# Two-layer hybrid encoder step on one core: the norms' sums taken by token, root and inverse on 128x5, the factors spread by the identity

## The chip, the core and the metric

The kernel runs on one core of a Trainium2 chip. The core's engines run their own instruction streams and meet at semaphores: TensorE (PE, with its weight loads shown apart as PEld), VectorE (DVE), ScalarE (ACT), GpSimd (POOL), and SyncE (SP), which issues the weight transfers. The metric is the device time of one launch in microseconds; before the change the median of three runs is 3305.26 us (3304.61 to 3308.02).

## The reference, cut to what matters

One inference step of a two-layer encoder over 512 prompt tokens and 64 sample tokens, 576 in all, with 1024 features. All in float32.

```
def rmsnorm(x, g):
    y = x * lax.rsqrt(jnp.mean(x * x, axis=-1, keepdims=True) + EPS)
    return y * g
# each of 2 layers:
h = x + 0.5 * rmsnorm(swiglu_1(rmsnorm(x)))           # FFN 1, inner width 2816
u = rmsnorm(h);  branch inputs, gate logits = u @ w_in
#   A  GLU -> causal depthwise conv (31) -> LayerNorm -> swish
#   B  HGRN2 gated linear recurrence; rmsnorm over each head's 64 features, * silu(g)
#   C  sliding-window attention      D  stick-breaking attention
y_n = o_n @ w_branch[n];  mix = (sum_n sigmoid(gate_n) * y_n) @ w_out
h = h + rmsnorm(mix)
h = h + 0.5 * rmsnorm(swiglu_2(rmsnorm(h)))           # FFN 2
h = h + rmsnorm((p @ ple_w) * sigmoid(rmsnorm(h) @ ple_gate_w))   # PLE
```

## The kernel before, in words

**Tiling.** Features lie on the partitions and tokens on the free axis: an activation is eight tiles of 128x576 (`KD = 8`, `T = 576`), and a pair of PSUM banks holds one tile as two halves of 288 (`pair(p)`), or as 512 + 64 (`flat(p)`). Every weight is streamed in units of 128x1024: SP brings `wraw`, ACT rounds it to `whi` (L551), POOL subtracts for the rest `wlo` (L1936), and PE makes three products of each 128x128 block with each half of a tile, high by high, high by low and low by high (`products`, L589).

**Norms.** Each layer has eight RMS norms over the 1024 features. The even ones (`norm_h`: F1PRE, MPRE, F2PRE, PPRE) take the residual `h`, tile by tile while it is still being added up by DVE and POOL (L812): ACT squares a tile, PE sums the squares over the partitions (`h_sums`). The odd ones (`norm_y`: F1POST, MPOST, F2POST, PPOST) take a projection's output: DVE adds the squares of seven tiles into `sqsum` (L785), and PE sums `sqsum` and the eighth tile. In both the sum is a product with `ones` as the 128x128 stationary operand and the squares as the moving one (L614), so that each of 128 partitions of a PSUM pair holds every token's sum. ACT takes the root of both 128x288 halves (L730), DVE their reciprocal (L791), both in place in PSUM, and DVE multiplies each tile by its gain and this pair (`dve_residual` L820, `dve_apply` L803). After `dve_apply`, ACT rounds to `u_hi`, and DVE and POOL make `u_lo` (L797), which the next products wait for.

**What fills the gaps.** A norm of a projection is mostly followed by a norm of the residual, with nothing between them for PE. `keep_clock(pe, n, bank)` (L606) issues n products of 128x128 that nobody reads: 8 behind the sums of a `norm_y` (not at F1PRE of layer 0 and F2POST), 10 behind those of a `norm_h`. At F2POST to PPRE, the four `e_tile`s of the layer's embedding product (L1798) stand between the sums instead. In the branches, pieces of the gate products (`pe_fill`) stand in the gaps.

**Branch norms.** The recurrence's norm is per head and 64 features: PE sums one 128x576 tile (`headones`, L599), ACT writes the roots to SBUF (L1070), DVE takes a reciprocal of 128x576 (L1147), applies it (L1149) and multiplies by the gate (L1150), for each of two tiles in turn. Behind that DVE builds the convolution's input `zc` with the 30 columns of history (L1254 to L1261), which PE had turned only after the norm (`pe_conv`), and PE turns the tails of `zc` for output (L1162). The convolution's LayerNorm goes through the same root and reciprocal of 128x576.

**Order.** Each engine's order is written out by hand. The layers run in a loop of two passes over one code, FFN 1's and FFN 2's up-projections in loops within; F1PRE of layer 0 takes its input from the transposed tokens.

## Time and profile before

| | us |
|---|---|
| median of three runs | 3305.26 |
| the profiled execution's own time | 3308.97 |
| its span in the trace | 3307.3 |
| PE busy in the span | 3126.9 (95%) |
| DVE, ACT, POOL busy | 1035.4, 1094.5, 1179.9 |
| mean granted clock of TensorE | 0.974 of full speed |

The span is cut into work by engine; several engines are busy at once. The profiled execution lies 3.7 us above the median, and 1.7 us of its time lie around the span. The mean granted clock below one says that in some stretches TensorE ran at the lower of its two levels, 0.50 in the rows below.

### The profile page before, as it was taken

To read this page: it belongs to the slowest core of one execution; us is meant where nothing else is said; L and a number is where in the kernel's file an instruction comes from. 1 tells how busy PE (TensorE), PEld (TensorE's weight loads), DVE (VectorE), ACT (ScalarE), POOL (GpSimd) and SP (SyncE) were. 2 spreads that over 40 slices of the span, in tenths; PEclk is the share of its full clock that TensorE was granted. 3 is DMA by queue.
4 is the path that set the end of the run, shared out by engine and by line. 5 is a ranking of instruction groups with operands and counts; after the bars stand their busy time and mean duration, and the time that the engine had idled before them with its cause. 6 is when DMAs were issued, how large, how long until landed. Compare 5 with 4: busy or idle time off the path is not lost.

```text
span 3307.3 us, 54560 instructions
## 1 busy us (share of the span) xinstructions
PE 3126.9 (95%) x23487; PEld 2989.7 (90%) x23487; DVE 1035.4 (31%) x1435; ACT 1094.5 (33%) x1544; POOL 1179.9 (36%) x564
## 2 busy tenths in 40 slices
PE   8999989899999899999899999898999998999988
PEld 7999989886799899998899999888867998999977
DVE  4111034744443411102331110349344424111024
ACT  3232232235433332322432322322354333233223
POOL 5434332231143443433343333323212434334333
PEclk9999999999999999999999999999999999999998
DMA  3222212221122122232212222222211221222211
GB/s 101 82 82 79 84 57 61 78 69 45 43 79 77 52 82 82 81 91 69 61 57 82 82 80 82 59 61 78 61 47 49 79 77 57 82 80 85 86 56 61
DMA packets 455953, 236.21 MB, mean 71 GB/s; under 512 B 18630, under 2 KB 454150, under 8 KB 455814
## 3 DMA queue, kind: packets, MB, share of 16 engines
q1 hardware_dynamic: 445792, 227.05, 23.5%
q10 hardware_dynamic: 10022, 7.15, 0.7%
q8 instruction: 107, 1.75, 0.2%
q14 instruction: 32, 0.26, 0.0%
HBM read 228.53 MB, written 5.63 MB: 71 GB/s over the span
## 4 chain that ended last, share of the span: by engine, by line
PE 86%; DVE 8%; ACT 3%; issue 1%; ACTq 1%; POOL 1%; POOLq 0%; DVEq 0%
PE ps L589 78%; PE ps L614 3%; DVE ps L791 2%; PE ps L1491 1%; DVE uf L803 1%; PE ps L1509 1%; PE ps L1471 1%; DVE u_lo L797 1%; DVE kgate L1103 0%; DVE roots L1147 0%; PE ps L1495 0%; ACT u_hi L719 0%; PE ps L1798 0%; POOL u_lo L797 0%; DVE uf L820 0%
## 5 line engine op out<-in xcount | busy, mean ns | idle before, releaser
L1936 POOL TENSOR_TENSOR wlo<-wraw,whi 128x1024 fp32r<-128x1024 f32 (+1 forms) x432 | 1043.1, 2419 | 1943.3 <-ACT whi L551 1943.1
L589 PE MATMUL ps<-u_hi,whi 128*128 128x288 f32 x4800 | 1053.5, 301 | 50.0 <-DVE u_lo L797 27.0
L589 PE MATMUL ps<-u_lo,whi 128*128 128x288 f32 x4800 | 1035.2, 297 | 0.0
L589 PE MATMUL ps<-u_hi,wlo 128*128 128x288 f32 x4800 | 1034.5, 297 | 0.0
L589 PEld LDWEIGHTS ps<-u_hi,whi 128*128 128x128 f32 x4800 | 778.6, 191 | 82.0 <-issue 54.3
L589 PEld LDWEIGHTS ps<-u_lo,whi 128*128 128x128 f32 x4800 | 781.6, 191 | 0.0
L589 PEld LDWEIGHTS ps<-u_hi,wlo 128*128 128x128 f32 x4800 | 780.5, 190 | 0.0
L551 ACT ACTIVATE whi<-wraw 128x1024 fp32r<-128x1024 f32 (+1 forms) x432 | 449.5, 1040 | 565.6 <-PE ps L589 332.0
L846 DVE TENSOR_TENSOR sq<-sq,ps 128x576 f32<-128x576 f32 x88 | 66.4, 754 | 901.5 <-PE ps L589 901.5
L589 PE MATMUL ps<-s_hi,whi 128*128 128x288 f32 x1408 | 301.9, 296 | 0.0
L589 PE MATMUL ps<-s_hi,wlo 128*128 128x288 f32 x1408 | 301.6, 296 | 0.0
L589 PE MATMUL ps<-s_lo,whi 128*128 128x288 f32 x1408 | 301.3, 296 | 0.0
L589 PEld LDWEIGHTS ps<-s_hi,whi 128*128 128x128 f32 x1408 | 226.9, 189 | 0.3
L589 PEld LDWEIGHTS ps<-s_lo,whi 128*128 128x128 f32 x1408 | 226.9, 189 | 0.0
L589 PEld LDWEIGHTS ps<-s_hi,wlo 128*128 128x128 f32 x1408 | 226.9, 189 | 0.0
L551 ACT ACT_TABLE_LOAD x44 | 56.5, 1283 | 420.7 <-PE ps L589 420.7
L785 DVE TENSOR_TENSOR sqsum<-sqsum,sq 128x576 f32<-128x576 f32 x54 | 40.8, 755 | 473.7 <-ACT sq L698 473.7
L1269 DVE SCALAR_TENSOR_TENSOR yc<-zc,taps_all,yc 128x606 f32<-128x606 f32 x120 | 142.5, 1189 | 4.2
L614 PE MATMUL ps<-sq,ones 128*128 128x288 f32 x260 | 87.5, 497 | 43.8 <-ACT sq L698 43.8
L698 ACT ACTIVATE sq<-ps 128x576 f32<-128x576 f32 x48 | 31.3, 652 | 280.8 <-PE ps L589 280.8
L614 PEld LDWEIGHTS ps<-sq,ones 128*128 128x128 f32 x260 | 57.1, 233 | 68.8 <-ACT sq L698 53.3
L791 DVE RECIPROCAL ps<-ps 128x288 f32<-128x288 f32 x32 | 62.9, 1966 | 131.8 <-ACT ps L730 131.3
(268 smaller groups left out, 2632.0 us busy)
## 6 DMA issues: line engine op xcount, KB each, us to landing
wraw<-in_ffn_up SPq DMA_DIRECT2D x176, 512.0 KB, 3.8
wraw<-in_w_in SPq DMA_DIRECT2D x104, 512.0 KB, 3.9
wraw<-in_ffn_down SPq DMA_DIRECT2D x64, 512.0 KB, 4.0
wraw<-in_ffn_down SPq DMA_DIRECT2D x32, 384.0 KB, 3.4
wraw<-in_w_out SPq DMA_DIRECT2D x16, 512.0 KB, 4.1
wraw<-in_ple_gate_w SPq DMA_DIRECT2D x16, 512.0 KB, 4.0
wraw<-in_w_branch SPq DMA_DIRECT2D x16, 256.0 KB, 2.7
xtok<-in_x_prompt SPq DMA_DIRECT2D x4, 512.0 KB, 7.1
```

What stands on the lines that cost most here:

```text
L551: act.activation(whi[:, i % SLOTS, 0:width(i)], wraw[:, i % SLOTS, 0:width(i)], ACT.Copy).then_inc(w_rounded, 1)
L589: ins = pe.matmul(ps[:, 2 * p + f, 0:HT], wt[:, part, w], x[:, k, HT * f:HT * f + HT], start=start and n == 0 and c == 0, stop=stop and n ...
L614: ins = pe.matmul(ps[:, 2 * norm_pair(n) + f, 0:HT], ones[:], x[:, HT * f:HT * f + HT], start=start, stop=stop)
L785: dve.tensor_tensor(sqsum[:], sqsum[:], sq[:, k % 2, :], ALU.add).then_inc(sq_added, 1)
L791: link(dve, dve.reciprocal(x, x))
L797: engine.tensor_tensor(u_lo[:, k, :], uf[:, k, :], u_hi[:, k, :], ALU.subtract).then_inc(signal, 1)
L803: dve.scalar_tensor_tensor(out=halves(uf[:, k, :]), in0=halves(h[:, k, :]), scalar=gains_all[:, n, L, k:k + 1], in1=pair(norm_pair(n)), op ...
L846: dve.tensor_tensor(halves(x), halves(x), pair(2 * q + 1), ALU.mult).then_inc(up_mul, 1)
L1269: ins = dve.scalar_tensor_tensor(out=yc[:, c, :], in0=zc[:, c, w:w + YW], scalar=wc, in1=yc[:, c, :], op0=ALU.mult, op1=ALU.add)
L1471: pe.matmul(ps[:, bk, 0:SEQ - 128 * kb], proj[hh, BK_ + c, 128 * kb:128 * kb + 128], proj[hh, BQ_ + c, 128 * kb:SEQ], start=True, stop=Tru ...
L1491: ins = pe.matmul(ps[0:nk, bk, 0:w], trineg[0:nk, 0:nk], spx[0:nk, i % 2, 0:w], start=False, stop=sb_first(i), skip_group_check=True)
L1936: pool.tensor_tensor(wlo[:, i % SLOTS, 0:width(i)], wraw[:, i % SLOTS, 0:width(i)], whi[:, i % SLOTS, 0:width(i)], ALU.subtract).then_inc( ...
```

## The change

**Sums.** The squares become the stationary operand, in five blocks of 128 tokens (the last one overlapping), and 64 columns of `ones` the moving one. A PSUM tile of 128 tokens x 64 equal columns comes out for each block, in the free part of the pair's second bank. Its first column is the sum by token.

**Root and inverse.** ACT takes the root of 128x5 into `rcol`, DVE the reciprocal of 128x5 in SBUF, and PE spreads it back to the layout that the apply reads: a column of `rcol`, repeated 128 times, is the stationary operand and the identity the moving one (`spread`), five products into the flat pair. DVE's apply waits for `factors_out`. Of the products that nobody reads, 2 now stand ahead of the wait for the reciprocal; behind it stand 8 (`norm_y`) and 6 (`norm_h`, 10 before).

**Branch norms.** The recurrence's norm sums both tiles, then turns the history (into bank 6), fills, and spreads both; its factors differ by head, so DVE copies them wide (128x640) first. DVE places the history between the two. The convolution's norm goes likewise, with its spread behind the first quarter of a gate unit, and the sliding-window part now waits for the norm's apply (`cv_norm`) where it waited for the root.

**Start.** Gains, taps and rows are copied from PSUM by ACT (8 instructions) where DVE did it (7 instructions in a chain, two of them scalings of gains).

```diff
-            def norm_sums(pe, n, x, start, stop):
-                for f in range(2):
-                    ins = pe.matmul(ps[:, 2 * norm_pair(n) + f, 0:HT], ones[:], x[:, HT * f:HT * f + HT], start=start, stop=stop)
...
+            SAME = 64
+            def sum_at(p):
+                return ps[:, 2 * p + 1, 64:64 + SAME * TB].rearrange("p (t s) -> p t s", t=TB)
+            def token_sums(pe, p, x, start, stop):
+                for tb in range(TB):
+                    t0 = min(128 * tb, T - 128)
+                    ins = pe.matmul(sum_at(p)[:, tb], x[:, t0:t0 + 128], ones[:, 0:SAME], start=start and tb == 0,
+                                    stop=stop and tb == TB - 1, skip_group_check=True)
                 return ins
+            def spread(pe, p, col):
+                for tb in range(TB):
+                    t0, n0 = 128 * tb, 0 if tb < TB - 1 else 64
+                    ins = pe.matmul(flat(p)[:, t0:t0 + 128 - n0], col(tb), ident[:, n0:128], start=True, stop=True)
+                return ins
+            def norm_factors(pe, n):
+                if n != N_F2POST:
+                    keep_clock(pe, 2, 2 if n % 2 else 6)
+                pe.wait_ge(rstd_ready, n + 1 + before(rstd_ready))
+                spread(pe, norm_pair(n), lambda tb: rcol[:, tb:tb + 1].to_broadcast([128, 128])).then_inc(factors_out, 1)
...
+                norm_factors(pe, n)
                 if n not in (N_F1PRE, N_F2POST):
                     keep_clock(pe, 8, 2)
...
-                keep_clock(pe, 10, 6)
+                norm_factors(pe, n)
+                keep_clock(pe, 6, 6)
...
             def act_root(act, n):
-                for f in range(2):
-                    act.wait_ge(norm_sum, 2 * n + f + 1 + before(norm_sum))
-                    x = ps[:, 2 * norm_pair(n) + f, 0:HT]
-                    act.activation(x, x, ACT.Sqrt, bias=eps_col[:], scale=1.0 / D).then_inc(std_ready, 1)
+                act.wait_ge(norm_sum, n + 1 + before(norm_sum))
+                act.activation(rcol[:], sum_at(norm_pair(n))[:, :, 0], ACT.Sqrt, bias=eps_col[:], scale=1.0 / D).then_inc(std_ready, 1)
...
             def dve_rstd(dve, n):
-                for f in range(2):
-                    dve.wait_ge(std_ready, 2 * n + f + 1 + before(std_ready))
-                    x = ps[:, 2 * norm_pair(n) + f, 0:HT]
-                    link(dve, dve.reciprocal(x, x))
+                dve.wait_ge(std_ready, n + 1 + before(std_ready))
+                dve.reciprocal(rcol[:], rcol[:]).then_inc(rstd_ready, 1)
+                dve.wait_ge(factors_out, n + 1 + before(factors_out))
...
-                    lk(dve.reciprocal(rstd[:], (std, sqsum)[c][:]))
+                    lk(dve.reciprocal(rhead[:, c], rhead[:, c]))
+                    dve.tensor_copy(rwide[:, c].rearrange("p t (a m) -> p t a m", a=2), rhead[:, c].unsqueeze(3).to_broadcast([128, TB, 2, 64])).then_inc(hg_rstd, 1)
...
             def pe_sw_tok(pe):
-                pe.wait_ge(cv_std, 1 + before(cv_std))
+                pe.wait_ge(cv_norm, 2 + before(cv_norm))
...
                 pe_hg(pe)
                 for c in range(2):
-                    hg_norm_pe(pe, c)
-                    pe_fill(pe, 2)
+                    hg_norm_sums(pe, c)
+                pe_conv_past(pe)
+                pe_fill(pe, 1)
+                for c in range(2):
+                    hg_norm_factors(pe, c)
+                pe_fill(pe, 3)
                 pe_conv(pe)
...
+                pe.wait_ge(rstd_ready, N_PPRE + 1 + before(rstd_ready))
+                spread(pe, norm_pair(N_PPRE), lambda tb: rcol[:, tb:tb + 1].to_broadcast([128, 128])).then_inc(factors_out, 1)
                 for j in range(5, KD):
                     e_tile(j)
```

How the instructions stand at three places. PE from FFN 1's output to the mixer's first product, before (L614 the sums, L606 `keep_clock`, L589 the weights' products) and after (L626 the sums, L634 `spread`, L611 `keep_clock`, L594 the weights' products):

```order
L614 MATMUL ps<-sqsum,ones 128x288 x2
L614 MATMUL ps<-sq,ones 128x288 x2
L606 MATMUL ps<-ident,ones 128x128 x8
L614 MATMUL ps<-sq,ones 128x288 x16
L606 MATMUL ps<-ident,ones 128x128 x10
L589 MATMUL ps<-u_hi,whi 128x288 x2
```

```order
L626 MATMUL ps<-ones,sqsum 128x64 x5
L626 MATMUL ps<-ones,sq 128x64 x5
L611 MATMUL ps<-ident,ones 128x128 x2
L634 MATMUL ps<-ident,rcol 128x128 x4
L634 MATMUL ps<-ident,rcol 128x64
L611 MATMUL ps<-ident,ones 128x128 x8
L626 MATMUL ps<-ones,sq 128x64 x40
L611 MATMUL ps<-ident,ones 128x128 x2
L634 MATMUL ps<-ident,rcol 128x128 x4
L634 MATMUL ps<-ident,rcol 128x64
L611 MATMUL ps<-ident,ones 128x128 x6
L594 MATMUL ps<-u_hi,whi 128x288 x2
```

The wait for DVE's reciprocal now stands on PE between two `keep_clock`s, and the eight unread products have moved behind it.

PE from FFN 2's last product to the embedding's first (`p_hi`), before and after:

```order
L589 MATMUL ps<-s_hi,wlo 128x288 x2
L614 MATMUL ps<-sqsum,ones 128x288 x2
L614 MATMUL ps<-sq,ones 128x288 x2
L1798 MATMUL ps<-p_hi,whi 128x288 x2
L1798 MATMUL ps<-p_lo,whi 128x288 x2
```

```order
L594 MATMUL ps<-s_hi,wlo 128x288 x2
L626 MATMUL ps<-ones,sqsum 128x64 x5
L626 MATMUL ps<-ones,sq 128x64 x5
L634 MATMUL ps<-ident,rcol 128x128 x4
L634 MATMUL ps<-ident,rcol 128x64
L1848 MATMUL ps<-p_hi,whi 128x288 x2
```

The embedding's products, which followed the sums at once, now stand behind the wait for the reciprocal.

DVE at the recurrence's norm (`of` its output, `zc` the convolution's input), before and after:

```order
L1147 RECIPROCAL roots<-roots 128x576
L1149 SCALAR_TENSOR_TENSOR of<-of,rows_all,roots 128x576
L1150 TENSOR_TENSOR of<-of,proj 128x576
L1147 RECIPROCAL roots<-sqsum 128x576
L1149 SCALAR_TENSOR_TENSOR of<-of,rows_all,roots 128x576
L1150 TENSOR_TENSOR of<-of,proj 128x576
L1254 MEMSET zc 128x2x30
L1256 COPY zc<-ps 128x2x30
L1260 TENSOR_TENSOR zc<-proj 128x512
L1261 TENSOR_TENSOR zc<-proj 128x64
```

```order
L1181 RECIPROCAL rhead<-rhead 128x10
L1182 COPY att<-rhead 128x640
L1297 MEMSET zc 128x2x30
L1299 COPY zc<-ps 128x2x30
L1181 RECIPROCAL rhead<-rhead 128x10
L1182 COPY att<-rhead 128x640
L1186 SCALAR_TENSOR_TENSOR of<-of,rows_all,ps 128x576
L1187 TENSOR_TENSOR of<-of,proj 128x576
L1186 SCALAR_TENSOR_TENSOR of<-of,rows_all,ps 128x576
L1187 TENSOR_TENSOR of<-of,proj 128x576
L1306 TENSOR_TENSOR zc<-proj 128x512
L1307 TENSOR_TENSOR zc<-proj 128x64
```

The history's two instructions have moved ahead of both applies, and the applies behind both reciprocals.

## Rows read from the trace of the kernel before

**Rows 1.** The page's busy times, share of the span and instructions by engine.

```profile
PE 3126.9 (95%) x23487; PEld 2989.7 (90%) x23487; DVE 1035.4 (31%) x1435; ACT 1094.5 (33%) x1544; POOL 1179.9 (36%) x564
```

**Rows 2.** Waits of PE: who waits, releaser, us in all, times, mean us.

```profile
PE ps L614 <- ACT sq L698: 43.8, 13, 5.3
```

**Rows 3.** Single lines: median, low and high ns of one; first to last start; forms.

```profile
L791 DVE RECIPROCAL ps<-ps x32: 1965/1966/1967, 24.0 to 3285.8; 128x288 f32<-128x288 f32 x32
L518 ACT ACTIVATE lb_work<-lb_work x1: 205/205/205, 39.3 to 39.3; 128x4 f32<-128x4 f32 x1
L496 DVE RECIPROCAL lb_work<-lb_work x1: 166/166/166, 39.9 to 39.9; 128x2 f32<-128x2 f32 x1
```

**Rows 4.** Timeline, PE, FFN 1 to mixer: start, length, instructions [idle before <- releaser].

```profile
456.93 1.17 PE L614 MATMUL ps<-sq,ones 128*128 128x288 f32 x4
457.93 1.95 PE L606 MATMUL ps<-ident,ones 128*128 128x128 f32 x16
465.13 1.32 PE L614 MATMUL ps<-sq,ones 128*128 128x288 f32 x2 [5.25 <-ACT sq L698]
...
482.64 0.82 PE L589 MATMUL ps<-u_hi,whi 128*128 128x288 f32 x2 [4.40 <-DVE u_lo L797]
```

**Rows 5.** Timeline, DVE, the same place.

```profile
458.15 3.97 DVE L791 RECIPROCAL ps<-ps 128x288 f32<-128x288 f32 x2 [18.16 <-ACT ps L730]
462.16 1.54 DVE L820 SCALAR_TENSOR_TENSOR uf<-y,gains_all,ps 128x576 f32<-128x576 f32 x2
...
470.49 1.13 DVE L812 TENSOR_TENSOR h<-h,uf 128x576 f32<-128x576 f32 x1
...
476.17 3.97 DVE L791 RECIPROCAL ps<-ps 128x288 f32<-128x288 f32 x2 [4.55 <-ACT ps L730]
```

**Rows 6.** Windows: stretch, length, busy us (instructions) by engine, granted clock, DMA share, GB/s.

```profile
463.60:470.40 6.80, 5.26 (x11) 3.84 (x12) 6.80 (x10) 2.73 (x4) 6.37 (x4) 0.50 0.00 0
866.40:868.90 2.50, 2.44 (x20) 1.71 (x18) 0.34 (x2) 2.44 (x5) 1.03 (x1) 1.00 0.47 136
869.80:871.00 1.20, 0.00 (x0) 0.00 (x0) 1.13 (x2) 0.00 (x0) 0.42 (x1) 0.50 0.01 4
1640.70:1642.90 2.20, 0.00 (x0) 0.00 (x0) 1.43 (x2) 2.17 (x3) 0.00 (x0) 1.00 0.32 92
```

**Rows 7.** Timeline, PE, f32 products of 128x128 in a row, at full clock and at half.

```profile
475.85 2.40 PE L606 MATMUL ps<-ident,ones 128*128 128x128 f32 x20
...
3290.16 0.87 PE L2017 MATMUL ps<-ident,h 128*128 128x128 f32 x3 [4.63 <-DVE h L812]
...
3294.82 1.54 PE L2017 MATMUL ps<-ident,h 128*128 128x128 f32 x6 [0.47 <-POOL h L812]
```

**Rows 8.** Timeline, PE and DVE, the recurrence's norm and the convolution's start, layer 0.

```profile
592.30 2.29 PE L599 MATMUL ps<-sq,headones 128*128 128x288 f32 x4 [5.74 <-ACT sq L1067]
595.47 3.75 DVE L1147 RECIPROCAL roots<-roots 128x576 f32<-128x576 f32 x1 [15.96 <-ACT roots L1070]
605.42 2.78 DVE L1150 TENSOR_TENSOR of<-of,proj 128x576 f32<-128x576 f32 x1
610.54 1.03 PE L1162 MATMUL ps<-ident,zc 128*30 128x128 f32 x4 [7.42 <-DVE zc L1261]
```

**Rows 9.** Timeline, PE, two of PPRE's pairs of sums, an embedding product between, layer 0.

```profile
1570.73 2.21 PE L614 MATMUL ps<-sq,ones 128*128 128x288 f32 x8 [2.25 <-ACT sq L698]
...
1575.85 2.21 PE L614 MATMUL ps<-sq,ones 128*128 128x288 f32 x8 [1.31 <-ACT sq L698]
```

**Rows 10.** Windows, columns as in rows 6: recurrence to convolution, F2POST to PPRE, dense products.

```profile
610.50:613.80 3.30, 3.25 (x15) 3.07 (x16) 3.13 (x5) 0.59 (x1) 0.00 (x0) 0.51 0.07 19
1556.80:1562.60 5.80, 5.80 (x16) 4.66 (x17) 5.76 (x8) 0.68 (x1) 5.54 (x4) 0.50 0.00 0
3272.00:3278.00 6.00, 6.00 (x47) 6.00 (x46) 1.43 (x2) 1.34 (x2) 0.00 (x0) 1.00 0.00 0
```

**Rows 11.** Timeline, PE, the first sums of the program.

```profile
18.84 2.26 PE L614 MATMUL ps<-sqsum,ones 128*128 128x288 f32 x4 [1.10 <-DVE sqsum L785]
```

More of the change, by code:

```diff
@@ L145, in trunk @@
         roots = keep("roots", [2 * T])
-        std, rstd = roots[:, 0:T], roots[:, T:2 * T]
+        rcol = keep("rcol", [TB])
+        rhead = keep("rhead", [2, TB, 2])
         u_at = keep.at
@@ L514, in setup_scalar, with rows_scalar @@
                           a["swa_sinks"].rearrange("(o l) h -> o (l h)", o=1).to_broadcast([128, 4 * DEPTH])).then_inc(rows_loaded, 16)
+        def rows_scalar(act):
+            act.wait_ge(turned, KD + 1)
+            g = gains_all[:].rearrange("p n l k -> p n (l k)")
+            rows = ps[:, ROW_BANKS[0], 0:128].rearrange("p (n x) -> p n x", n=8)
+            for n0, n1, c in ((N_F1PRE, N_F1POST, 1.0), (N_F1POST, N_MPRE, 0.5), (N_MPRE, N_F2POST, 1.0), (N_F2POST, N_PPRE, 0.5), (N_PPRE, 8, 1.0)):
+                act.activation(g[:, n0:n1], rows[:, n0:n1], ACT.Copy, scale=c).then_inc(rows_kept, 1)
+            act.activation(taps_all[:].rearrange("p l w -> p (l w)"), ps[:, ROW_BANKS[1], 0:N_TAPS], ACT.Copy).then_inc(rows_kept, 1)
+            act.activation(rows_all[:, 0:N_ROWS - 4], ps[:, ROW_BANKS[2], 0:N_ROWS - 4], ACT.Copy).then_inc(rows_kept, 1)
+            act.activation(lb_work[:, 0:4], ps[:, ROW_BANKS[2], N_ROWS - 4:N_ROWS], ACT.Copy).then_inc(rows_kept, 1)
+            act.wait_ge(rows_kept, 8)
         def bounds_scalar(act):
@@ L742, in act_ffn @@
                         act_round(act, k - (KD - 2))
+                if f == 0 and L == 0:
+                    rows_scalar(act)
                 act_norm_root(act, 4 * f + N_F1PRE)
@@ L802, in dve_apply @@
                 for k in range(KD):
-                    dve.scalar_tensor_tensor(out=halves(uf[:, k, :]), in0=halves(h[:, k, :]), scalar=gains_all[:, n, L, k:k + 1],
-                                             in1=pair(norm_pair(n)), op0=ALU.mult, op1=ALU.mult).then_inc(u_full, 1)
+                    dve.scalar_tensor_tensor(out=uf[:, k, :], in0=h[:, k, :], scalar=gains_all[:, n, L, k:k + 1],
+                                             in1=flat(norm_pair(n)), op0=ALU.mult, op1=ALU.mult).then_inc(u_full, 1)
                     if k and k - 1 in LO_DVE:
@@ L1049, in act_hg, with hg_norm_sums, hg_norm_factors @@
                 act_fill(act, 6)
-            def hg_norm_pe(pe, c):
+            def hg_norm_sums(pe, c):
                 pe.wait_ge(hg_sq, 2 + before(hg_sq))
-                ones_product(pe, 2 + c, headones[:], sq[:, c, :]).then_inc(hg_ss, 1)
+                for tb in range(TB):
+                    t0 = min(128 * tb, T - 128)
+                    ins = pe.matmul(sum_at(2 + c)[:, tb], sq[:, c, t0:t0 + 128], headones[:, 32:96], start=tb == 0,
+                                    stop=tb == TB - 1, skip_group_check=True)
+                ins.then_inc(hg_ss, 1)
+            def hg_norm_factors(pe, c):
+                pe.wait_ge(hg_rstd, c + 1 + before(hg_rstd))
+                spread(pe, 2 + c, lambda tb: rwide[:, c, tb, :]).then_inc(hg_norm, 1)
             def act_hg_out(act, L):
@@ L1069, in act_hg_norm @@
                     act.wait_ge(hg_ss, c + 1 + before(hg_ss))
-                    act.activation(halves((std, sqsum)[c][:]), pair(2 + c), ACT.Sqrt, bias=eps_col[:], scale=1.0 / HD).then_inc(hg_std, 1)
+                    act.activation(rhead[:, c], sum_at(2 + c).rearrange("p t (a s) -> p t a s", a=2)[:, :, :, 0], ACT.Sqrt, bias=eps_col[:],
+                                   scale=1.0 / HD).then_inc(hg_std, 1)
                 act_fill(act, 4)
@@ L1175, in pe_conv @@
                 pe.wait_ge(cv_out, 1 + before(cv_out))
-                for t0, t1 in ((0, SEQ), (SEQ, T)):
-                    for c in range(2):
-                        ins = pe.matmul(flat(3)[:, t0:t1], ones[:], sq[:, c, t0:t1], start=c == 0, stop=c == 1)
+                for c in range(2):
+                    ins = token_sums(pe, 3, sq[:, c, :], c == 0, c == 1)
                 ins.then_inc(cv_var, 1)
-                pe_kept_gate(pe, GATES_CONV - 1)
+                g = GATES_CONV - 1
+                pe_gate_free(pe, g)
+                for j in range(4):
+                    unit_part(pe, U0_GATE + g, j, g % 2, QUARTERS)
+                    if j == 0:
+                        pe.wait_ge(cv_rstd, 1 + before(cv_rstd))
+                        spread(pe, 3, lambda tb: rcol[:, tb:tb + 1].to_broadcast([128, 128])).then_inc(cv_fac, 1)
             PROJ_CONV = FILL0 + (16 + 2 + TB + 4 + 1 + 4) // 4 - 1
@@ L1280, in dve_conv @@
                 dve.wait_ge(cv_std, 1 + before(cv_std))
-                lk(dve.reciprocal(rstd[:], std[:]))
+                dve.reciprocal(rcol[:], rcol[:]).then_inc(cv_rstd, 1)
+                dve.wait_ge(cv_fac, 1 + before(cv_fac))
                 dve.wait_ge(cv_xc, 2 + before(cv_xc))
@@ L1706, in pe_mixer @@
                 for c in range(2):
-                    hg_norm_pe(pe, c)
-                    pe_fill(pe, 2)
+                    hg_norm_sums(pe, c)
+                pe_conv_past(pe)
+                pe_fill(pe, 1)
+                for c in range(2):
+                    hg_norm_factors(pe, c)
+                pe_fill(pe, 3)
                 pe_conv(pe)
@@ L1754, in dve_mixer @@
                 dve_hg(dve)
-                dve.wait_ge(hg_std, 2 + before(hg_std))
                 dve_conv(dve)
```

69 lines of the change are left out of this document (33 added, 36 removed).

## The prediction, as put on record before the result

> **What bounds the kernel now.** First the page's busy times: PE is busy for 95% of the span, no other engine for more than 36% [rows 1]. The dense weight products are not touched by this change, so what it can win or lose lies in the 5% and in stretches in which PE runs at half clock. Second, PE's waits: the largest that the change touches is for the residual's first squares, 43.8 us in 13 waits [rows 2]. Third, the timelines around one such place. The last sums of FFN 1's output start at 456.93, unread products follow until 459.9, and PE then has nothing for 5.25 us [rows 4]. The time goes to DVE: two reciprocals of 1.97 us each [rows 3], 458.15 to 462.12, and only then the first apply at 462.16 [rows 5]. At the norm behind it the same pair stands at 476.17, and PE waits 4.40 us for the first product [rows 4, 5]. Fourth, windows with the granted clock: behind the gap it is 0.50, that is 1.2 instead of 2.4 GHz, from 463.6 to 470.4 [rows 6]. There are five such pairs of norms (FFN 1 to mixer twice, mixer to FFN 2 twice, layer 0's PLE to layer 1's FFN 1), two stretches with embedding products between the sums (F2POST to PPRE), two recurrence and two convolution norms, the start and the end.
>
> **The chain of one norm.** Before, from the last sums' start to the first apply: 462.16 - 456.93 = 5.23 us [rows 4, 5]. After, first the price of a small f32 product. Each leaves two records. 20 records take 2.40 us and 16 take 1.95 [rows 4, 7], so one more costs (2.40 - 1.95)/4 = .11 us at full clock; at half, six take 1.54 and three .87 [rows 7], or .22, twice as much. A product of 64 columns is shorter only in its moving part, not in its 128-column weights: I take the 128x128 price, bounds from half of it to all of it. Then ten records of sums 10 x .11 + .27 for the last one's way out = 1.4; a root of 128x5 like ACT's 128x4, .205, and a reciprocal like DVE's 128x2, .166 [rows 3]; `spread`, ten records, 1.4; four hand-overs of about .05 each (the gap from reciprocals to apply is .04 [rows 5]). Sum 3.3, so a gain of 1.9 at full clock. At half clock sums and spread cost 1 us more each, and it is gone. The two unread products ahead of the wait hide under root and reciprocal; the eight behind it take the place of those that stood there.
>
> **A pair, clock held.** -1.9 at the first norm. In the second, the last residual tile is added at 470.49 + 1.13 = 471.6, yet the reciprocals come at 476.17 [rows 5], since the sums ran late at half clock; at full clock a tile's ten records (1.1) keep up with DVE and POOL, and I count -1.5 of the 4.5. Then -1.9 again: **-5.3**. Whoever counts all of the 4.5 gets more, but u_lo behind the apply limits PE by then.
>
> **A pair, clock lost.** PE's gap shrinks from 5.25 to about 5.25 - 1.9 - 2 = 1.4, because the eight products now stand later. Whether the clock falls in that is the case's main question. If it does, it may stay down: a tile's sums cost ten small records at .22 = 2.2 against four of 288 columns, .48 each at half (1.32 for two [rows 4]) = 1.9. A row here speaks for it staying down: from 866.4 to 868.9 PE was busy 2.44 of 2.50 us, with small products, and at 869.8 the clock stood at .50 [rows 6]. Six tiles that cannot recover cost 6 x (2.2 - 1.9) = +1.8, and up to +3.3 with the spread of the second norm at half and the later recovery. I take **+2**. For holding: a gap of 2.2 us from 1640.7, between dense products, kept 1.00 [rows 6]. The evidence is about even, and it will depend on where the gap falls, pair by pair. Half of five: 2.5 x -5.3 + 2.5 x 2 = **-8.2**.
>
> The Trainium skill, in "TensorE: Matmul & The Clock Gate", section "Why this matters for your kernels", advises to leave no idle gaps between bursts of matmuls. By that rule a gap cut to 1.4 us would hold the clock everywhere, which is the first rival; the trace agrees at 1640.7, and at 869.8 it does not [rows 6].
>
> **F2POST to PPRE, two.** Here the embedding's first two products, which followed the sums at once, now wait behind the reciprocal, with no unread products to cover it: PE stands still for about .6 us, and they cost their place, +.3. Two chains -2.0 each, the half-clock stretch of 5.8 us [rows 10] costs -2.9 if gone, of which I count -1.9 as PE is not last in all of it; eight sums of 10 records in place of 4 +1.1; -1.0 for a start without a gap: **-5.5** if the clock holds. But each of three turns (now 5.12 us, 1570.73 to 1575.85 [rows 9]) has two sums: at half clock 20 x .22 = 4.4 against 8 x .24 = 1.9 (eight take 2.21 with the last one's way out [rows 9]), and 12 rows of the embedding product at twice .13 (47 in 6.00 us [rows 10]), +1.5. That is +4 a turn, 3 x 4 - 5.5 = +6.5 for all. The clock is at half before the first turn already [rows 10], and the one row on small products shows none under which it rose [rows 6]. I take 2.1 turns: **+3 each, +6**.
>
> **Recurrence, two.** Sums of both tiles from 592.30 at half clock, 20 x .22, to 596.7; one fill unit, 12 rows at .26, to 599.8; both spreads, 10 at half and 10 at full, to 603.1. DVE's work meanwhile shrinks by its reciprocal of 3.75 [rows 8] for each tile, against a short one and a copy. Two applies and gate products to about 605 (.8 each; beside POOL one took 2.78 [rows 8], bound +2), the GLU of `zc` 1.8 more to 606.7; the fills, 36 rows at .13, end at 607.7. PE's tail turn stands at 610.54 behind 7.42 us of idle [rows 8]: -2.8. With the gap the 3.3 us at half clock behind it [rows 10] go: -1.6. **-4.4 each, -8.8**. The history's transposes cost nothing, under DVE's wait; without that cover .3.
>
> **Convolution, two.** The chain is covered by a gate unit; the shorter reciprocal frees DVE, but the sliding-window part now waits for the applies (two of about .8) where it waited for the root. Bounds -2 and +1, I take **-.4 each**, nearest to nothing, since the last kept gate stands beside it.
>
> **Start and end.** Sums at 18.84 [rows 11], two reciprocals from 24.0 [rows 3], behind DVE's copies of gains, apply at 28.0. After: ACT takes eight copies (some .28 each, 2.2 us) behind its last rounding at 19.9, root and reciprocal to 22.6, spread at half 2.1, apply at 24.8: **-3.2**; bounds -1.6 (copies at .5) and -4.1. At the end -1.9 for the chain, and the gap of 4.63 before the output's transposes, which run at half [rows 7], becomes about 2: -1.0, **-2.9**.
>
> The waits that are new have nothing else behind them: PE's holds unread products, or the embedding's as counted, DVE's only its own applies. No transfer moves past another.
>
> **The sum.** -8.2 + 6 - 8.8 - .8 - 3.2 - 2.9 = -17.9. The profiled execution took 3308.97 (span 3307.3), so 3291.1 for one like it; it lies 3.7 above the median, so **3287**, -0.54%.
>
> **Rivals.**
> 1. *The clock holds everywhere.* 5 x -5.3 - 11.0 - 8.8 - .8 - 3.2 - 2.9 = -53.2: **3252**. For it the held gap of 2.2 us; against it the small products ahead of 869.8 [rows 6].
> 2. *Slower: the clock falls in every stretch and stays down through the sums.* Pairs at their bound, 5 x 3.3 = +16.5; PPRE +13; recurrence without the clock's part -5.6; conv -.8, start -3.2, end -1.9: +18, **3323**. It decides from where all pairs are lost and all turns run at half; at +2 a pair it is +11.5, 3317. For it, that sums of 64 columns take 10 records where 4 stood; against it the shorter gap.
> 3. *The change does not shorten the chain.* If each of the four hand-overs takes .5 us, the new chain is 3.3 + 1.8 = 5.1 and no norm gains; with recurrence at half its gain and the rest at nothing, about -2 to +3: **3303 to 3308**. Against it the .04 us between reciprocal and apply [rows 5].
>
> **How the numbers follow.** Forecast .55, rival 1 .17, rival 2 .20, rival 3 .08. A measurement of this kernel can tell about 0.2%, 6.6 us, from no change: faster is below 3298.7, slower above 3311.9. Faster: .52 of the forecast's .55, and rival 1: .69. Same: .03 of the forecast, rival 3, .04 of rival 2's low edge: .15. Slower: the rest of rival 2, .16. The range runs from rival 1's 3250 to 3317, the lower end of rival 2; outside are half of rival 2 and the low edge of rival 1, under .2.
>
> **What would show it.** In the changed trace the reciprocal's line at about .17 us, PE's gap in a pair at 1.4, and the first apply 3.3 us behind the last sums show the chain; the granted clock over the residual's sums and records of .11 or .22 us decide forecast against rivals 1 and 2, the latter if it is .50 in all five pairs and all turns. PE's idle time ahead of the convolution's tails should all but vanish, and the first apply come near 24.8. If some pairs hold and others don't, times should scatter more than the 3.4 us of before. Wrong would be a chain over 4.5 us, or spread and sums at prices of other sizes.

## The result, and the profile after

The changed kernel takes 3280.85 us (median of four runs, 3279.12 to 3285.45), the kernel before 3305.28 in the same comparison: a ratio of 0.9924, 95% interval 0.9912 to 0.9936. The profiled execution took 3279.91, its span is 3278.2. The forecast was 3287 and its range 3250 to 3317, so time and sign came out as forecast. The terms under the sum did not all do so, the largest least of all, and half of what follows is about that.

The page of the changed kernel, busy times by engine as in [rows 1]:

```profile
span 3278.2 us, 55957 instructions
PE 3162.7 (96%) x24207; PEld 3049.5 (93%) x24207; DVE 958.7 (29%) x1417; ACT 1079.8 (33%) x1536; POOL 1179.9 (36%) x564
```

PE is busy 36 us longer in a span that is 29 us shorter: there are 720 more records, and its idle time shrank. Four of its waits, as in [rows 2] (us in all, times, longest; the last number is the longest wait there too, and not the mean):

```profile
PE ps L626 <- ACT sq L722: 18.3, 13, 2.3
...
PE ps L1078 <- ACT sq L1098: 11.5, 2, 5.7
...
PE ps L594 <- DVE u_lo L819: 6.4, 8, 1.1
PE ps L626 <- DVE sqsum L809: 5.8, 3, 2.3
```

Two more of the kernel before:

```profile
PE ps L589 <- DVE u_lo L797: 27.0, 6, 5.0
PE ps L1162 <- DVE zc L1261: 15.2, 2, 7.7
```

The wait for the residual's first squares went from 43.8 to 18.3 us, that for `u_lo` behind a norm of the residual from 27.0 to 6.4, and the 15.2 us ahead of the convolution's tails are gone. Those ahead of the recurrence's sums (11.5) and of a projection's sums (5.8) are as they were. Now the two profiles stage by stage, each stage from the first record of one PE group to the first record of the next, worked out from PE's timelines:

| stage | before | after | difference | forecast |
|---|---|---|---|---|
| start: first sums to first product | 11.62 | 9.72 | -1.9 (and +.35 ahead of it) | -3.2 |
| five pairs: projection's sums to next product | 26.68, 27.14, 27.13, 26.21, 26.37 | 21.23, 21.21, 24.02, 21.21, 21.21 | -24.7 | -8.2 |
| mixer's first product to convolution's tails, two | 127.90, 127.92 | 125.83, 125.80 | -4.2 | -5.6 |
| tails to the product behind the convolution's mean, two | 101.04, 100.85 | 99.56, 99.56 | -2.8 | -3.2 |
| from there to the mixer output's sums, two | 381.75, 382.73 | 379.20, 381.86 | -3.4 | -.8 |
| F2POST's sums to PPOST's, two | 95.36, 94.76 | 98.51, 98.46 | +6.9 | +6 |
| PPOST's sums to the end | 25.74 | 26.42 | +.7 | -2.9 |
| the rest (both FFNs) | | | 0 | 0 |

Together -29.1, the difference of the two spans. The medians differ by 24.4, since the run of before that was profiled lies 3.7 us above its median and that of the changed kernel .9 below.

PE from FFN 1 to the mixer's first product, the place of [rows 4], after:

```profile
454.40 1.23 PE L626 MATMUL ps<-ones,sqsum 128*128 128x64 f32 x10
455.46 1.28 PE L626 MATMUL ps<-ones,sq 128*128 128x64 f32 x10
456.58 0.66 PE L611 MATMUL ps<-ident,ones 128*128 128x128 f32 x4
457.32 1.33 PE L634 MATMUL ps<-ident,rcol 128*128 128x128 f32 x10
458.49 2.00 PE L611 MATMUL ps<-ident,ones 128*128 128x128 f32 x16
461.67 9.45 PE L626 MATMUL ps<-ones,sq 128*128 128x64 f32 x80 [1.18 <-ACT sq L722]
```

and DVE there, the place of [rows 5]:

```profile
457.08 0.19 DVE L813 RECIPROCAL rcol<-rcol 128x5 f32<-128x5 f32 x1 [18.64 <-ACT rcol L752]
458.69 1.54 DVE L842 SCALAR_TENSOR_TENSOR uf<-y,gains_all,ps 128x576 f32<-128x576 f32 x2 [1.42 <-PE ps L634]
...
471.55 0.19 DVE L813 RECIPROCAL rcol<-rcol 128x5 f32<-128x5 f32 x1 [3.38 <-ACT rcol L752]
```

The chain from the last sums to the first apply is 458.69 - 455.46 = 3.23 us where it was 5.23; 3.3 was forecast. PE's gap is 1.18 where it was 5.25 [rows 4]. And the eighty records of the residual's sums take 9.45 us, because the clock held. Windows (stretch, length, busy us and instructions of PE, PEld, DVE, ACT, POOL, granted clock, DMA share, GB/s) of these sums, of layer 0's sums at PPOST, and two of the later turns of F2POST to PPRE:

```profile
461.70:471.10 9.40, 9.40 (x81) 9.25 (x82) 6.43 (x8) 4.79 (x7) 8.42 (x5) 1.00 0.00 0
1627.10:1633.50 6.40, 6.40 (x30) 6.40 (x31) 0.19 (x1) 2.23 (x4) 0.00 (x0) 0.50 0.13 39
1544.80:1548.20 3.40, 3.40 (x16) 3.27 (x15) 0.00 (x0) 0.00 (x0) 0.00 (x0) 0.50 0.00 0
1551.60:1566.00 14.40, 12.41 (x57) 11.88 (x55) 0.19 (x1) 2.06 (x4) 0.84 (x1) 0.50 0.01 2
```

At 1627.1 the clock fell ahead of the sums, in an idle stretch of 2.29 us like the one that had held in [rows 6] at 1640.7; this is the pair of 24.02, and the same happens at the end. From 1544.8 to 1548.2 it is down while PE is busy throughout, and from 1551.6 for more than a turn. PE's timeline there, where two turns of before are [rows 9]:

```profile
1537.33 2.44 PE L626 MATMUL ps<-ones,sq 128*128 128x64 f32 x20 [1.31 <-ACT sq L722]
...
1542.74 2.70 PE L626 MATMUL ps<-ones,sq 128*128 128x64 f32 x20 [1.31 <-ACT sq L722]
...
1550.63 3.67 PE L626 MATMUL ps<-ones,sq 128*128 128x64 f32 x20 [2.26 <-ACT sq L722]
...
1558.61 4.53 PE L626 MATMUL ps<-ones,sq 128*128 128x64 f32 x20 [1.31 <-ACT sq L722]
```

A turn takes 5.41 us at full clock (1537.33 to 1542.74) and 7.9 and 8.0 behind that, the first partly and the second nearly all at half: the twenty records go from 2.44 to 4.53 us, and the embedding's products behind them take longer too.

### The profile page after: what moved, and what is told of

It reads as the page before. It is cut to its first block, busy times and chain, and to the rows that moved or that the text cites. A ratio compares the mean times of both kernels' runs of the same rounds, so it can differ in the third digit from the quotient of the medians.

```text
span 3278.2 us, 55957 instructions
## 1 busy us (share of the span) xinstructions
PE 3162.7 (96%) x24207; PEld 3049.5 (93%) x24207; DVE 958.7 (29%) x1417; ACT 1079.8 (33%) x1536; POOL 1179.9 (36%) x564
## 4 chain that ended last, share of the span: by engine, by line
PE 89%; DVE 5%; ACT 3%; POOL 1%; issue 1%; ACTq 1%; POOLq 0%; DVEq 0%
PE ps L594 79%; PE ps L626 3%; PE ps L634 1%; PE ps L1538 1%; PE ps L1848 1%; DVE uf L825 1%; PE ps L1556 1%; PE ps L1518 1%; DVE u_lo L819 1%; POOL u_lo L819 1%; ACT u_hi L743 0%; DVE kgate L1135 0%; PE ps L1542 0%; PE ps L1527 0%; DVE att L1153 0%
## 5 line engine op out<-in xcount | busy, mean ns | idle before, releaser
L594 PE MATMUL ps<-u_hi,whi 128*128 128x288 f32 x4800 | 1051.4, 300 | 37.5 <-ACT ybr L1714 11.8
L594 PE MATMUL ps<-u_lo,whi 128*128 128x288 f32 x4800 | 1033.8, 296 | 0.0
L594 PE MATMUL ps<-u_hi,wlo 128*128 128x288 f32 x4800 | 1033.3, 296 | 0.0
L594 PEld LDWEIGHTS ps<-u_hi,whi 128*128 128x128 f32 x4800 | 770.2, 189 | 72.6 <-issue 32.9
L594 PEld LDWEIGHTS ps<-u_hi,wlo 128*128 128x128 f32 x4800 | 774.1, 189 | 0.0
L594 PEld LDWEIGHTS ps<-u_lo,whi 128*128 128x128 f32 x4800 | 774.0, 189 | 0.0
L594 PE MATMUL ps<-s_hi,whi 128*128 128x288 f32 x1408 | 303.1, 296 | 0.0
L594 PE MATMUL ps<-s_hi,wlo 128*128 128x288 f32 x1408 | 302.7, 296 | 0.0
L594 PE MATMUL ps<-s_lo,whi 128*128 128x288 f32 x1408 | 302.5, 296 | 0.0
L594 PEld LDWEIGHTS ps<-s_hi,wlo 128*128 128x128 f32 x1408 | 226.5, 189 | 0.0
L594 PEld LDWEIGHTS ps<-s_lo,whi 128*128 128x128 f32 x1408 | 226.5, 189 | 0.0
L594 PEld LDWEIGHTS ps<-s_hi,whi 128*128 128x128 f32 x1408 | 226.2, 189 | 0.3
L1315 DVE SCALAR_TENSOR_TENSOR yc<-zc,taps_all,yc 128x606 f32<-128x606 f32 x120 | 150.5, 1256 | 4.2
L626 PE MATMUL ps<-ones,sq 128*128 128x64 f32 x690 | 93.3, 297 | 18.3 <-ACT sq L722 18.3
L626 PEld LDWEIGHTS ps<-ones,sq 128*128 128x128 f32 x690 | 89.8, 211 | 22.1 <-ACT sq L722 21.4
L594 PE MATMUL ps<-m_split,whi 128*128 128x288 f32 x512 | 89.4, 296 | 0.3 <-DVE m_split L1746 0.3
```

The costliest lines, as they stand in the source:

```text
L594: ins = pe.matmul(ps[:, 2 * p + f, 0:HT], wt[:, part, w], x[:, k, HT * f:HT * f + HT], start=start and n == 0 and c == 0, stop=stop and n ...
L626: ins = pe.matmul(sum_at(p)[:, tb], x[:, t0:t0 + 128], ones[:, 0:SAME], start=start and tb == 0, stop=stop and tb == TB - 1, skip_group_ch ...
L1315: ins = dve.scalar_tensor_tensor(out=yc[:, c, :], in0=zc[:, c, w:w + YW], scalar=wc, in1=yc[:, c, :], op0=ALU.mult, op1=ALU.add)
```

## The experiments

Three theories stood at first. A: a pair gains half by the shorter chain and half by the clock, which the eight products behind the spread hold. B: all is the clock. C: all is the shorter chain.

**The kernel before, its gaps filled.**

```diff
-                    keep_clock(pe, 8, 2)
+                    keep_clock(pe, 26, 2)
...
-                keep_clock(pe, 10, 6)
+                keep_clock(pe, 24, 6)
```

> The kernel before, with more unread products in the two gaps of a pair: 26 behind the sums of a projection's norm (8 before), 24 behind those of the residual's (10 before); sums, roots and reciprocals as they were. Theory A (half the gain of a pair is the clock, half the shorter chain): with the clock held the residual's sums keep up, the second reciprocals come about 2 us earlier in each of five pairs, but 3.97 us of reciprocals stay in both chains: about 3294. Theory B (all is the clock): near the changed kernel, 3281. Theory C (all is the shorter chain): no change, 3305.

3299.83 against 3306.02, ratio 0.9988 (0.9975 to 1.0000). DVE at the first pair of this kernel:

```profile
458.52 3.97 DVE L791 RECIPROCAL ps<-ps 128x288 f32<-128x288 f32 x2 [18.16 <-ACT ps L730]
...
474.70 3.97 DVE L791 RECIPROCAL ps<-ps 128x288 f32<-128x288 f32 x2 [2.71 <-ACT ps L730]
```

The second reciprocals come 16.2 us behind the first ones, where it was 18.0 [rows 5], and every one of the five pairs takes 24.9 us (24.85 in the first, 481.17 - 456.32). So with the old sums the held clock is worth about 1.9 us a pair, and the short chain the rest, 24.9 to 21.2: a third and two thirds, where theory A had halves. B and C are out. The split is that of a kernel which keeps the clock; with the new sums the clock is worth more, as the next run shows. The total fell short of 3294 as the pairs gave 9.3 us in all, not 11, and as the kernel before is at 3306.0 in this comparison, not at the 3309 of its profiled execution. Alone it would show little: the 21 runs of the kernel before lie between 3294.59 and 3310.60 here, and the interval reaches 1.0000. The reading rests on the five pairs in the trace.

**The changed kernel without the eight products behind the spread.**

```diff
-                if n not in (N_F1PRE, N_F2POST):
-                    keep_clock(pe, 8, 2)
```

> The changed kernel without the eight unread products behind the spread of a projection's norm. Theory A: PE's gap ahead of the residual's sums grows from 1.18 to about 3 us, the clock falls in it and the sums of small products run at half, five pairs lose 4 to 7 us each: 3301 to 3316. Theory C (the shorter chain alone holds the clock): 3281, within 3 us.

3320.22 (3318.13 to 3320.64), ratio to before 1.0045 (1.0031 to 1.0059): slower than the kernel before. PE's timeline at the first pair:

```profile
457.80 1.33 PE L634 MATMUL ps<-ident,rcol 128*128 128x128 f32 x10
462.14 16.46 PE L626 MATMUL ps<-ones,sq 128*128 128x64 f32 x80 [3.02 <-ACT sq L720]
```

A window of the same stretch, columns as above:

```profile
462.20:478.00 15.80, 15.80 (x79) 15.72 (x79) 6.39 (x8) 4.78 (x7) 8.37 (x5) 0.54 0.00 0
```

All five pairs lost the clock and take 28.8, 30.2, 32.6, 30.1 and 30.2 us, 7.6 to 11.4 above a held one. That is more than the 4 to 7 expected of theory A, and the total lies above its range, but its sign holds; C falls. The shorter chain alone does not hold the clock, and without the clock it is no gain: a lost pair costs 2 to 5.5 us more than before the change. The row to remember is the window: PE is busy in 15.80 of 15.80 us, with no gap, and stays at about half clock.

**F2POST to PPRE filled; PPOST filled.** Ahead of the sums of residual tiles 0, 2, 4 and 6 in the one, ahead of the sums of PPOST in the other:

```diff
                 for k in range(KD):
+                    if k % 2 == 0:
+                        keep_clock(pe, 10 if k == 4 else 6, 2)
                     h_sums(pe, N_PPRE, k)
```

```diff
                 pe.wait_ge(ple_sig, 6 + before(ple_sig))
+                keep_clock(pe, 10, 2)
                 pe_norm_y(pe, N_PPOST)
```

> The changed kernel with unread products in the idle stretches of F2POST to PPRE, ahead of the sums of residual tiles 0, 2 and 6 (six each) and 4 (ten). Theory A: the stretch got 3.2 and 3.7 us longer since it runs at half clock from the second turn on; with the clock held turns of 7.9 us become 5.4 and the end of the stretch 1.5 shorter: -6.5 a layer, 3268. Rival (the turns are set by the ring of ACT's squares and copies and PE's sums, whatever the clock): within 2 us of 3281.

> The changed kernel with ten unread products ahead of the sums of PPOST, where PE waits 2.29 us for DVE. Theory A: the profile of the changed kernel shows the clock fallen in that gap in both layers, with the sums behind it at half; filled, layer 0's pair comes to the 21.2 us of the other four from 24.0 and the end gets 2 to 3 us shorter: 3276. Rival (the gap holds as often as not, and the filling only delays the sums): 3281 or up to 1 us more.

The first: 3270.43 (3269.60 to 3278.01), 0.9896 (0.9874 to 0.9918). F2POST to PPOST takes 91.0 us in both layers where the changed kernel had 98.5: -7.5, a little over the -6.5 expected; the rival falls. But in this profile two pairs that had held, the second and the fourth, take 28.80 and 28.54 us. PE's timeline in the second:

```profile
1085.49 2.00 PE L611 MATMUL ps<-ident,ones 128*128 128x128 f32 x16
1088.67 16.37 PE L626 MATMUL ps<-ones,sq 128*128 128x64 f32 x80 [1.18 <-ACT sq L722]
```

A window in these sums:

```profile
1090.10:1107.10 17.00, 17.00 (x80) 16.99 (x81) 5.22 (x7) 4.36 (x7) 7.28 (x4) 0.50 0.00 0
```

The same 1.18 us of gap, behind the same sixteen unread records, that held at 461.67 in the changed kernel, did not hold here. So a gap of 1.2 us with small products behind it may go either way, and a pair is at 21.2 or some 7.5 above that. What decides it, no run here shows.

The second: 3278.93, but ten runs from 3269.73 to 3305.71, ratio 0.9932 (0.9908 to 0.9957). In the profile (3271.08) layer 0's pair takes 21.32 (24.02 before), and PPOST to the end's first transposes 6.74 (9.47): -2.7 each, as expected; with such a scatter the median settles nothing. That runs of one kernel lie 36 us apart is in keeping with up to five pairs that hold or not, at some 7.5 us each. The mean granted clock, on record for each run, goes with the time: .984 and .985 in the three runs up to 3271.1, .977 and .978 in the two at 3291, .972 in the one at 3305.7. So the scatter goes with the clock; that it lies in the pairs is argued, since only the one run was profiled.

**All filled.** Both of the above, and `keep_clock(pe, 14, 2)` for 8 behind the spread, which closes the 1.18 us:

> The changed kernel with all idle stretches around its norms filled: fourteen unread products behind the spread of a projection's norm (8 before), the four places of F2POST to PPRE and the one ahead of PPOST. Theory A (each pair either holds the clock, 21.2 us, or loses it, 28 to 33 us, by where the remaining 1.18 us fall): all five pairs at 21.2, no run above the others, 3264 to 3266 with a spread under 3 us. Rival (the scatter has another source, and filled gaps only delay the sums): the median of the changed kernel with unread products at F2POST to PPRE alone, 3270, and runs 8 us apart.

3258.88, ratio 0.9856 (0.9840 to 0.9873), four runs from 3258.33 to 3259.37. All five pairs take 21.21 to 21.32, F2POST to PPOST 90.9. PE at the first pair:

```profile
458.65 3.34 PE L611 MATMUL ps<-ident,ones 128*128 128x128 f32 x28
461.82 1.33 PE L626 MATMUL ps<-ones,sq 128*128 128x64 f32 x10
```

The sums start 4.34 us behind the spread's start (457.48), with the gap they did so 4.35 behind it (457.32): the filling costs nothing. The scatter is gone, 1.0 us where it had been 6 to 36 (and 12.6 in the kernel with 88 columns below, run in the same comparison), so its source is in the gaps that were filled. It is 5 us below what was expected, since that was reckoned from the kernel with F2POST to PPRE filled, whose runs had lost pairs in them.

**How many equal columns.** `SAME = 64` to 88 and to 8 in the changed kernel, the recurrence's sums kept at 64:

> The changed kernel with sums in 88 equal columns (64 before; the recurrence's stay at 64). Price of a record: if the weights set it, .11 us as now. If the columns serve the clock, pairs hold at least as often and F2POST to PPRE recovers: 3270 to 3279. If columns do nothing but take time: 3281 to 3286.

> The changed kernel with sums in 8 equal columns (the recurrence's stay at 64); the number that is used of them is one. If the weights set the price of a record, .11 us as now and nothing is saved. If the columns serve the clock, it falls in most of the five pairs and stays down through the sums: +8 each, 3300 to 3325. If they don't: 3281, and if they cost time 3270.

88 columns: 3273.12 (3263.73 to 3276.33), ratio 0.9893 (0.9874 to 0.9911). 8 columns: 3322.65 (3322.03 to 3324.36), 1.0050 (1.0033 to 1.0066). The same ten records, each at 454 us of its kernel, with 88 columns:

```profile
454.31 1.25 PE L630 MATMUL ps<-ones,sqsum 128*128 128x88 f32 x10
```

and with 8:

```profile
454.70 1.18 PE L630 MATMUL ps<-ones,sqsum 128*128 128x8 f32 x10
```

The price of a record hardly depends on the columns: 1.18, 1.23 and 1.25 us for ten at 8, 64 and 88. A single column would give the same sums, and the others are not used; yet with 8 all five pairs take 26.9 to 31.0 us. Two windows of the first of them:

```profile
454.70:458.20 3.50, 3.47 (x31) 3.28 (x30) 0.19 (x1) 2.36 (x4) 0.00 (x0) 1.00 0.55 154
458.20:461.60 3.40, 3.40 (x18) 3.40 (x18) 2.12 (x3) 0.04 (x1) 0.50 (x1) 0.50 0.00 0
```

Here the clock fell at 458.2, while PE was busy with the sums and the products behind them, with no gap before it or behind it; with 64 columns the same stretch kept it. With 88 the four pairs that held before hold, and layer 1's F2POST to PPOST holds too, at 90.9 where layer 0's takes 98.5; whether the columns did that or the chance of one profile is not shown.

**Parts of the change taken back.** These stand on the kernel with all filled, whose 1 us of scatter lets a few us be seen (the kernel before is at 3306.17 in its comparison and at 3306.33 in that of the later ones). First the recurrence's norm and the history as before the change (`hg_norm_pe`, reciprocals of 128x576, `pe_fill(pe, 2)` behind each sum, history in `pe_conv`):

> As the kernel with all stretches filled, but with the recurrence's norm and the convolution's history as they were before the change. The prediction counted this part at -4.4 a layer, the traces of before and after give -3.5 (2.1 to the convolution's tails, 1.4 at half clock behind them): 3264 + 7 = 3271. Rival (the DVE chain of the convolution behind it takes it all back): 3265.

3268.50 (3266.58 to 3270.15) against 3258.88: +9.6. To the tails it is 2.8 and 2.0 us longer, from there to the product behind the convolution's mean .3 and 2.5, and most of the rest lies in half-clock stretches behind it. PE's timeline at the tails shows the gap of [rows 8] again:

```profile
604.31 1.04 PE L1185 MATMUL ps<-ident,zc 128*30 128x128 f32 x4 [7.24 <-DVE zc L1289]
```

So this part is worth 7 to 10 us, as forecast (-8.8). Then the start:

```diff
-                if f == 0 and L == 0:
-                    rows_scalar(act)
...
+            link(dve.tensor_copy(gains_all[:].rearrange("p n l k -> p (n l k)"), ps[:, ROW_BANKS[0], 0:128]))
...
```

> As the kernel with all stretches filled, but gains, taps and rows are copied by DVE again. The prediction counted -3.2 for the start, partly from these copies off DVE's chain; the traces show -1.6, and before the change DVE's copies ended at 23.96 where the changed kernel's root ends at 24.06. Theory: the copies are hidden behind the sums at half clock, the first apply comes at most .4 us later: 3259, within 1 us. Rival (they were on the path): 3261 to 3262.

3257.72 (3255.73 to 3259.68) against 3258.88. DVE at the start of this kernel:

```profile
18.80 4.32 DVE L481 TENSOR_SCALAR gains_all<-gains_all 128x16 f32<-128x16 f32 x2
...
23.88 0.19 DVE L814 RECIPROCAL rcol<-rcol 128x5 f32<-128x5 f32 x1
26.56 1.54 DVE L826 SCALAR_TENSOR_TENSOR uf<-h,gains_all,ps 128x576 f32<-128x576 f32 x2 [2.49 <-PE ps L637]
```

The first apply comes 7.85 us behind the first sums (18.71), and with the copies on ACT 7.65 behind them (26.60, 18.95). DVE's copies end .3 us behind the root (23.84, 23.52), so moving them gave .2 us at most, which the totals can't show. Then the convolution's norm:

```diff
-                pe.wait_ge(cv_norm, 2 + before(cv_norm))
+                pe.wait_ge(cv_std, 1 + before(cv_std))
```

(and root, reciprocal and sums of 128x576 as before)

> As the kernel with all stretches filled, but with the convolution's norm as before the change (root and reciprocal of 128x576, and the sliding-window part waiting for the root). The prediction counted -.4 a layer for it, within -2 and +1. From the convolution to the mixer's output the profiles of before and after differ by 2.6 and .9 us, but half-clock stretches behind it, which fall by chance, are in that. Theory A: 3260, within 1 us. Theory B (the gap ahead of the sliding-window products, 4.1 before and 2.3 after, is this norm's): 3262 to 3263.

3255.47 (3255.31 to 3256.43): 3.4 us faster without this part of the change. PE at the sliding-window part, with the norm as before the change:

```profile
714.65 0.27 PE L1341 MATMUL ps<-ident,swk_c 128*128 128x128 f32 x1
...
720.20 0.69 PE L1361 MATMUL ps<-proj 64*128 64x64 f32 x4 [4.08 <-ACT swk_tok L1402]
```

and with the new one, in the kernel with all filled:

```profile
716.68 0.27 PE L1346 MATMUL ps<-ident,swk_c 128*128 128x128 f32 x1
...
720.43 0.44 PE L1366 MATMUL ps<-proj 64*128 64x64 f32 x4 [2.28 <-ACT swk_tok L1407]
```

The wait of 4.08 us became 2.28, which looks like a gain, but the turns ahead of it start 1.2 us later, counted from the product behind the convolution's mean. They don't wait for `cv_norm`: PE has no idle time ahead of them, and `spread`'s ten records in its stream take most of the 1.2. The products behind the wait start 19.96 us after the product behind the convolution's mean, and 20.57 with the old norm: .6 us, not 1.8. Neither theory had the sign of the total. From the last kept gate to the mixer output's sums the new norm takes 370.4 and 373.1 us and the old one 372.4 and 370.4: better in one layer, worse in the other. The clock is at half for 13.7 and 17.1 us of these with the new norm, and for 17.1 and 10.2 with the old one, and goes with the times. So the norm itself is about nothing, and what differs is where the clock falls behind it; why it falls there was not tried.

**Embedding's products ahead of the wait.** As before the change, on the kernel with all filled:

```diff
+                if n == N_F2POST:
+                    return
...
                 e_tile(0)
                 e_tile(1)
+                norm_factors(pe, N_F2POST)
```

> As the kernel with all stretches filled, but at F2POST the embedding's first two products stand ahead of the wait for the reciprocal, as before the change, and the spread behind them. Theory: PE's .6 us of waiting goes, but spread and first apply come 2.5 us later and the residual's sums with them: 3263 to 3264. Rival (POOL's first addition, which stands behind a weight unit's subtraction, sets the sums' start either way): 3257 to 3260.

3260.77 (3260.13 to 3262.49), +1.9. The first apply comes 2.4 us later behind the sums (6.67 for 4.29), but the residual's sums only .9 (9.64 for 8.78). ACT there with the spread ahead (`e` is its copy of an embedding product):

```profile
1535.29 0.65 ACT L1888 ACTIVATE e<-ps 128x576 f32<-128x576 f32 x1 [0.93 <-PE ps L1848]
1535.84 1.25 ACT L722 ACTIVATE sq<-h 128x576 f32<-128x576 f32 x2
```

and with the products ahead:

```profile
1533.97 0.65 ACT L1891 ACTIVATE e<-ps 128x576 f32<-128x576 f32 x1 [0.92 <-PE ps L1850]
1537.28 0.68 ACT L724 ACTIVATE sq<-h 128x576 f32<-128x576 f32 x1 [2.65 <-DVE h L836]
```

The theory has the sign, and about half of the size; the rival has the reason wrong. DVE's first addition ends at 1534.45 with the spread ahead and at 1537.24 with the products ahead. ACT's first square comes 1.4 us behind it in the one, since the copy of the second embedding product stands in front of it, and at once in the other. So the new order is the better one, and ACT's copy takes 1.4 of its 2.4 us back. POOL's weight subtraction ahead of its first addition costs .2: that addition starts at 1533.79, and its input was ready at 1533.61.

**The recurrence's gap filled.** 24 unread products ahead of `hg_norm_sums`, in a bank whose reader is waited for:

```diff
+                pe.wait_ge(proj_out, FILL0 + 6 + before(proj_out))
+                keep_clock(pe, 24, 2 * ((FILL0 + 7) % 2))
                 for c in range(2):
                     hg_norm_sums(pe, c)
```

> As the kernel with all stretches filled, with 24 more unread products in PE's 5.7 us of idle ahead of the recurrence's sums. There the clock is at half for 10.2 us (profile of the changed kernel 13.7 and 10.2), sums take 4.5 and both spreads 3.6 us. Theory: at full clock sums, one fill unit and spreads are 2.1 + 1.5 + 1.2 us shorter, and the convolution's tails come 4 us earlier: 3251. Rival (DVE's work ahead of the tails sets the time): 3257 to 3259.

3252.36 (3252.11 to 3253.22), ratio 0.9837 (0.9820 to 0.9853): the fastest of all, 28 us under the changed kernel, and the rival falls. PE there:

```profile
579.80 5.52 PE L611 MATMUL ps<-ident,ones 128*128 128x128 f32 x48
585.70 2.44 PE L1078 MATMUL ps<-headones,sq 128*128 128x64 f32 x20 [0.38 <-ACT sq L1098]
...
589.99 2.34 PE L634 MATMUL ps<-ident,att 128*128 128x128 f32 x20
597.00 0.60 PE L1200 MATMUL ps<-ident,zc 128*30 128x128 f32 x4
```

In the changed kernel the same sums take 4.53 us and the spreads 3.65, and the tails stand 16.2 us behind the sums; here 11.3.

## Why the prediction was right, and where it was not

The total of -18 us against -24.4 in the medians is a sum of terms that missed in both directions, so that it came so near is in part luck: by the profiles the pairs gave 16.5 us more than forecast and the other terms 5.3 less, and the profiles differ by 4.7 more than the medians. Point by point, in its order:

- **The chain of one norm**: 3.3 forecast, 3.23 measured. Right, with its parts: the record at .11 us, whether 8, 64 or 88 columns; the reciprocal .19 where .17 was taken; the root .27 where it was .205.
- **A pair, clock held**: -5.3 forecast, -5.0 to -5.9 measured in four pairs. Right.
- **A pair, clock lost**: +2 taken, bound +3.3. The two that lost it behind a gap of 1.18 us, in the kernel with F2POST to PPRE filled, are at +1.7 and +2.3 (28.80, 28.54): right. The five without the eight products are at +2 to +5.5, three of them above the bound, but behind gaps of some 3 us, which it was not made for.
- **Half of five hold.** This is the step that failed. The gap came as forecast, 1.18 us for 1.4, but in the profile four pairs held throughout; the fifth lost the clock not in the gap that was forecast but in the 2.29 us ahead of its first sums, had it again for the residual's, and still gained 3.1. The term is -24.7 for -8.2. The reasoning that either could happen was right, as the runs with lost pairs show, but nothing in the trace of before gave the share. It is a term that varies from run to run.
- **F2POST to PPRE**: +6 forecast, +6.9 measured, by the mechanism put, with sizes that made up for each other. In layer 0 the two turns with the clock at half in them take 1.9 and 2.9 us more than those in their place before (4 a turn forecast) and the stretch behind the last sums 1.4 more; against that stand -.4 for the first chain and -2.5 for the first turn, now at full clock (-5.5 forecast).
- **Recurrence**: -8.8 forecast, -7.0 between the profiles, -9.6 by taking it back. Right, with its sign: PE's idle time ahead of the tails is gone.
- **Convolution**: -.4 a layer forecast; between the profiles -3.4 for the stretch of both layers, but taking it back shows no gain. Nearly nothing was right. The difference of the profiles comes with the clock behind it: kernels with this same norm take 379.0 to 382.9 us for layer 0's stretch.
- **Start**: -3.2 forecast, -1.6 measured. Two mistakes. ACT's eight copies were put at 2.2 us and take .8; and of the norm's two sets of ten records only one was counted, although `pe_norm_y` issues both behind the wait there. At half clock the twenty take 4.3 us where eight of 288 columns had taken 4.0.
- **End**: -2.9 forecast, +.7 measured. The chain is shorter, but the clock fell ahead of the sums of PPOST, in the 2.29 us that had held in [rows 6]. The forecast took that row as a sign that such a gap holds; filled, it comes back to -2.7 against the changed kernel.

Of the rivals, the first (the clock holds everywhere, 3252) is not the kernel that was predicted, but the one with all filled, at 3259; that this one reaches 3252 with the recurrence's gap filled is another gain, which the rival did not count. The second (slower, 3323) is near the changed kernel without the eight products, 3320, in which all five pairs lose the clock. The third falls with the chain of 3.23 us. The rule that the prediction cited, from "TensorE: Matmul & The Clock Gate" of the Trainium skill, section "Why this matters for your kernels", advises against idle gaps between bursts. The filled kernels agree: their pairs take 21.2 to 21.4 us. But that a gap of 1.4 us would hold everywhere, as the prediction took from it, does not come out: gaps of 1.18 held in all five pairs of the changed kernel and lost the clock in two of another. Nor does it cover the window above, in which PE had no idle time in 17.00 us and stayed at .50.

## What to carry to other kernels

A factor that is needed once per token belongs on a small tile: turn the operands of its sum so that root and reciprocal work on 128x5 instead of 128x576, and spread the result back with the identity. But price the new products at both clocks, since a chain that is 2 us shorter is worth less than the clock (7.6 to 11.4 us a pair here), and many small products may leave PE at half clock though it never waits. Where a kernel's runs scatter, look for a gap that sometimes costs the clock and fill it, and measure parts of a change only then.

## What the runs showed of the hardware that was not expected

- PE busy for 17.00 of 17.00 us at a granted clock of .50 (eighty small records of sums), where the same records at 461.7 run at 1.00: where it had fallen it stayed down to their end.
- The moving columns of these small f32 products cost next to nothing: ten records take 1.18 us with 8 columns, 1.25 with 88. But with 8 columns all five pairs lose the clock, the first of them at 458.2 with no gap before it, and the kernel is at 3322.65, with 64 at 3280.85.
- The same idle stretch of 2.29 us held the clock in the profile of before and lost it in that of the changed kernel, as the one of 1.18 us did between two pairs of one kernel.
